# Gated delta stage of a two-block transformer kernel: PSUM banks assigned as a ring, and the next head's preparation moved beside the scan

## What is computed

```
def _gated_delta_chunked(q, k, v, g, beta):
    L = where(strict, einsum(k_beta, k) * decay, 0)
    t_inv = triangular_solve(eye + L, eye)
    u, w = t_inv @ v_beta, t_inv @ (k_beta * exp(g))
    qk = where(tri, einsum(q, k) * decay, 0)
    def step(S, xs):                       # one chunk after the other
        v_new = u_c - w_c @ S
        o = qg_c @ S + qk_c @ v_new
        S = S * dl_c + kd_c^T @ v_new
o = o_fwd + o_bwd;  o = rms_norm(o) * silu(z)
```

## Time and profile before

| | us |
|---|---|
| median of 3 runs (4356.33 to 4364.41) | 4357.08 |
| the profiled execution | 4365.17 |
| its span in the trace | 4363.4 |
| delta stage, from the first level batch (2079.7) to o ready (2738.1) | 658.5 |
| PE busy over the whole span | 3933.6 (90%) |
| DVE busy | 2020.1 (46%) |
| ACT busy | 1886.3 (43%) |
| POOL busy | 1091.2 (25%) |
| mean granted clock of TensorE | 0.946 |

### The profile page before, as it was taken

How to read it: one execution, slowest core, us unless ns; L and a number is a source line. 1 busy time by engine, 2 the same in 40 slices (tenths; PEclk the granted TensorE clock), 3 DMA queues, 4 the chain that set the end, 5 groups by cost and what they waited for, 6 DMA issues and landing times. The chain is left out here.

```text
span 4363.4 us, 54559 instructions
## 1 busy us (share of the span) xinstructions
PE 3933.6 (90%) x20807; PEld 3314.5 (76%) x20807; DVE 2020.1 (46%) x3497; ACT 1886.3 (43%) x3241; POOL 1091.2 (25%) x596
## 2 busy tenths in 40 slices
PE   8989998879959999995878776897999999999998
PEld 6879997757737777874878775797888778888886
DVE  4358874277745222313656567674234233000353
ACT  5248765357746554331434443565324242111232
POOL 0034430010022332211333334122532111212341
PEclk9999998789979999997989887898999999999999
DMA  3744214489954322222221212114643123222342
GB/s 118 258 130 105 51 40 154 173 338 420 420 218 132 97 95 97 74 92 74 54 76 41 77 52 76 52 37 139 221 148 116 44 81 124 80 66 82 128 145 101
DMA packets 337172, 548.35 MB, mean 126 GB/s; under 512 B 117092, under 2 KB 210148, under 8 KB 325860
## 3 DMA queue, kind: packets, MB, share of 16 engines
...
## 5 line engine op out<-in xcount | busy, mean ns | idle before, releaser
L3340 POOL TENSOR_TENSOR end_w_lo<-end_w_raw,end_w_hi 128x1024 fp32r<-128x1024 f32 x144 | 353.6, 2465 | 835.8 <-ACT end_w_hi L3529 835.6
L3772 PE MATMUL end_ps<-end_xT_hi,end_w_hi 128*128 128x512 f32 (+1 forms) x896 | 344.7, 385 | 4.7 <-DVE end_xT_lo L3369 2.4
L3772 PE MATMUL end_ps<-end_xT_lo,end_w_hi 128*128 128x512 f32 (+1 forms) x896 | 342.9, 383 | 0.0
L3772 PE MATMUL end_ps<-end_xT_hi,end_w_lo 128*128 128x512 f32 (+1 forms) x896 | 342.8, 383 | 0.0
L3529 ACT ACTIVATE end_w_hi<-end_w_raw 128x1024 fp32r<-128x1024 f32 x144 | 150.1, 1054 | 268.4 <-PE end_ps L3772 139.9
L2685 POOL TENSOR_TENSOR mid_w_lo<-mid_w_raw,mid_w_hi 128x1024 fp32r<-128x1024 f32 (+1 forms) x64 | 153.0, 2396 | 406.3 <-ACT mid_w_hi L2873 406.3
L3043 PE MATMUL mid_ps<-mid_w_hi,mid_xT_hi 128*128 128x512 f32 x576 | 228.7, 397 | 2.8 <-DVE mid_xT_lo L2747 2.8
L3043 PE MATMUL mid_ps<-mid_w_lo,mid_xT_hi 128*128 128x512 f32 x576 | 224.4, 390 | 0.0
L3043 PE MATMUL mid_ps<-mid_w_hi,mid_xT_lo 128*128 128x512 f32 x576 | 224.4, 390 | 0.0
L3501 DVE TENSOR_TENSOR end_rows<-end_rows,end_ps 128x512 f32<-128x512 f32 x44 | 30.3, 688 | 417.5 <-PE end_ps L3772 417.5
L3772 PE MATMUL end_ps<-end_w_hi,end_xT_hi 128*128 128x512 f32 x544 | 214.4, 394 | 0.0
...
## 6 DMA issues: line engine op xcount, KB each, us to landing
...
```

The lines of the kernel that those rows point to most:

```text
L3340: pool.tensor_tensor(halves(w_lo, piece), w_raw[:, 2 * q:2 * q + 2], halves(w_hi, piece).bitcast(F32), ALU.subtract).then_inc(w_split, 1)
L3772: ins = pe.matmul(o_, lhsT, rhs, start=(k == 0 and part == 0), stop=(k == KC - 1 and part == 2))
```

## The change

- The level batches, and the u and w groups after them, use banks 0 to 4 in a ring: batch i writes bank i mod 5. Bank 5 is free for the preparation, banks 6 and 7 belong to the scan alone (the first head still prepares in 6 and 7). o shares its place with the product for v_new.
- The Gram products of head w+1 move from i = 16, 18, ... to i = 0, 3, 6, 9, beside the scan, each followed on DVE by its `decays` at i = 1, 4, 7, 10. `AQ` gets a third buffer; the freed tile `row_prod` moves into it.
- The transposes of k and v move to i = 24 to 27, all in bank 5, each waiting for ACT's copy of the one before (at i = 25 to 28).
- The elimination moves from i = 30 to 35 to i = 16 to 25, and so does what follows it on SP.
- `spread` and `exponents` run for head w+2 at i = 28 to 35, not for head w+1 beside the scan; those of head 1 run before the first turn.
- SP stores o and loads z ahead of `give_blocks`, not at the end of its turn.
- ACT squares the last o tiles one chunk at a time (i = 10 to 16), `root` moves to i = 22, `decay_rows` to i = 23.

```
-        L, AQ, inv = (st.sb(n, [P, 2, NI, P]) for n in ("L", "AQ", "inv"))
+        L, inv = (st.sb(n, [P, 2, NI, P]) for n in ("L", "inv"))
+        AQ = st.sb("AQ", [P, 3, NI, P])
...
-        turn_bank, half_bank, full_bank = (0, 1, 2, 3), (4, 5, 0, 1), (2, 3, 4, 5)
-        uw_bank = (0, 1, 2, 3, 4, 5, 2, 3)
-        uw_left = (1, 2, 7, 8)
+        RING = 5
+        uw_left = (5, 6, 7, 8)
...
-        PREP = SCANS
+        GRAM_AT, TURN_AT, KEEP_AT = (0, 3, 6, 9), (24, 25, 26, 27), (25, 26, 27, 28)
+        DECAY_AT, SQUARE_AT, SPREAD_AT, EXP_AT = (1, 4, 7, 10), (10, 12, 14, 16), (28, 29, 30, 31), (32, 33, 34, 35)
+
+        def prep_bank(h, j):
+            return 6 + j % 2 if h == 0 else 5
+
+        def scan_place(d, part):
+            return ps[:, 6 + d, part * P:(part + 1) * P]
+
+        def ring_bank(lev, phase, b):
+            return (((lev - 1) * 3 + phase) * NB + b) % RING
+
+        def uw_bank(g):
+            return (BATCHES + g) % RING
 
         def level_of(i):
...
                         if w + 2 < H:
                             load_rows(w + 2)
+                        if w:
+                            store(w - 1)
+                            load_z(w)
                         give_blocks(w + 1)
                         if w + 2 < H:
                             load_qk(w + 2)
...
-                    if w:
...
-                            dve.wait_ge(sd_done, NI * (h - 1))
+                        if h >= 3:
+                            dve.wait_ge(sd_done, NI * (h - 2))
...
+                for b in range(NB):
+                    spread(1, b)
...
-                SOLVED_AT = {BATCHES - 6: range(1, 4), BATCHES - 5: range(4, 7), BATCHES - 4: range(7, 9), BATCHES - 3: range(9, 11),
-                             BATCHES - 2: range(11, 13), BATCHES - 1: range(13, SMALL - 1)}
+                SOLVED_AT = {17: (1, 2), 18: (3, 4), 19: (5, 6), 20: (7,), 21: (8,), 22: (9,), 23: (10,), 24: (11, 12), 25: (13, 14)}
...
-                        if w and i == BATCHES - 10:
+                        if w and i == 26:
                             finish(w - 1)
                         if w + 1 < H:
-                            if i in (2, 5, 8, 11):
-                                spread(w + 1, i // 3)
-                            if PREP < i <= PREP + 4:
-                                decays(w + 1, i - PREP - 1)
-                            if i == BATCHES - 6:
+                            if i in DECAY_AT:
+                                decays(w + 1, DECAY_AT.index(i))
+                            if i == 16:
                                 begin_solve(w + 1)
                             if i in SOLVED_AT:
                                 solve(w + 1, SOLVED_AT[i])
+                            if w + 2 < H and i in SPREAD_AT:
+                                spread(w + 2, SPREAD_AT.index(i))
                         elif i < ROW_STEPS:
                             row_step(i)
                 for c in range(NT):
...
-                def squares(h):
-                    act.wait_ge(o_kept, NI * (h + 1))
-                    for t in range(NT):
-                        ins = act.activation(dump[:, t], o[:, t], ACT.Square, accum_out=osum[:, 0, t:t + 1])
-                    ins.then_inc(osum_done, 1)
+                def squares(h, c):
+                    for d in range(2):
+                        t = chunk_at(c, d)
+                        act.wait_ge(o_kept, NI * h + 2 * c + d + 1)
+                        act.activation(dump[:, t], o[:, t], ACT.Square, accum_out=osum[:, 0, t:t + 1]).then_inc(osum_done, 1)
 
...
-                        if w and i == PREP + 1:
-                            squares(w - 1)
-                        if w and i == PREP + 3:
+                        if w and i in SQUARE_AT:
+                            squares(w - 1, NT // 2 + SQUARE_AT.index(i))
+                        if w and i == 22:
                             root(w - 1)
                         if w + 1 < H:
-                            if i in (4, 7, 10, 13):
-                                exponents(w + 1, i // 3 - 1)
-                            if PREP + 4 < i <= PREP + 8:
-                                keep_tok(w + 1, i - PREP - 5)
-                            if i == BATCHES - 6:
+                            if i == 23:
                                 decay_rows(w + 1)
+                            if i in KEEP_AT:
+                                keep_tok(w + 1, KEEP_AT.index(i))
+                            if w + 2 < H and i in EXP_AT:
+                                exponents(w + 2, EXP_AT.index(i))
...
-                def prepare(h, i):
-                    j = i % 4
-                    if i == 0:
+                def gram(h, j):
+                    if j == 0:
                         pe.wait_ge(qk_in[h % 2], 32 * (h // 2 + 1))
-                        if h >= 2:
-                            pe.wait_ge(S_done, NI * (h - 1))
-                            pe.wait_ge(o_kept, NI * (h - 1))
                         if h:
                             pe.wait_ge(tok_done, 4 * h)
-                    if 2 <= i < 6:
-                        pe.wait_ge(grams_kept, 4 * h + i - 1)
-                    if i >= 6:
-                        pe.wait_ge(tok_done, 4 * h + i - 5)
-                    if i < 4:
...
+                    if h:
+                        pe.wait_ge(grams_kept, 4 * h + j)
+                    elif j >= 2:
+                        pe.wait_ge(grams_kept, j - 1)
+                    for n in range(2):
+                        t = 2 * j + n
+                        ins = pe.matmul(ps[:, prep_bank(h, j), n * 256:n * 256 + 256], qk[:, h % 2, t, 0],
+                                        qk[:, h % 2, t].rearrange("p m c -> p (m c)"), start=True, stop=True)
+                    ins.then_inc(grams, 1)
+
+                def turn_values(h, j):
+                    if h:
+                        pe.wait_ge(grams_kept, 4 * h + 4)
+                        pe.wait_ge(tok_done, 4 * h + j)
+                    elif j < 2:
+                        pe.wait_ge(grams_kept, j + 3)
                     else:
...
+                        pe.wait_ge(tok_done, j - 1)
+                    if j == 2:
+                        pe.wait_ge(v_in, 16 * (h + 1))
+                    for n in range(4):
+                        t = 4 * (j % 2) + n
+                        src = qk[:, h % 2, t, 0] if j < 2 else vT[:, t * P:(t + 1) * P]
+                        ins = turn(pe, bank(prep_bank(h, j))[:, n], src, ident)
+                    ins.then_inc(turned, 1)
...
-                        if w + 1 < H and PREP <= i < PREP + 8:
-                            prepare(w + 1, i - PREP)
+                        if w + 1 < H and i in GRAM_AT:
+                            gram(w + 1, GRAM_AT.index(i))
+                        if w + 1 < H and i in TURN_AT:
+                            turn_values(w + 1, TURN_AT.index(i))
                     pe.wait_ge(bvk_done, 4 * (w + 1))
                     for b in range(NB):
...
                     for b in range(NB):
-                        pe.wait_ge(lev_D, PER * w + NB * (LEVELS - 1) + (b + 1 if b < 2 else NB))
-                        if b == 3:
-                            pe.wait_ge(uw_copied, 8 * w + 4)
...
+                        for m in range(2):
+                            g = 2 * b + m
+                            pe.wait_ge(lev_D, PER * w + NB * (LEVELS - 1) + min(max(b + 1, g), NB))
+                            if g >= RING:
+                                pe.wait_ge(uw_copied, 8 * w + g - RING + 1)
+                            for k in range(4 * b, 4 * b + 4):
+                                left, right = ((kbg, invT) if m else (invT, bv))
+                                ins = pe.matmul(bank(uw_bank(g))[:, k % 4], left[:, k], right[:, k], start=True, stop=True)
+                            ins.then_inc(uw_done, 1)
```

95 lines of the change are left out of this document (41 added, 54 removed).

## The result

The changed kernel takes 4371.38 us (median of 12 runs), the kernel before 4363.77 us in runs on the same chip: a ratio of 1.0016, 95% interval 1.0009 to 1.0023. It is slower by 7.6 us, in the band that the forecast called "the same". In the profiled executions it is 6.7 us of span (4370.1 against 4363.4), and the delta stage holds more than all of it. Windows of the changed kernel: head 0, heads 1 to 6, the last head to its scan's end, and from there to TensorE's next work; then two stretches inside head 4. The columns are those of the earlier trace rows.

A forecast was written before the change was run, and what follows sets the result against it. Some 20 us a head of waits, latencies and slow clock above PE's 53 us of work. Head 0 +2.2, heads 1 to 6 -7.1, last head -3.3, end -1.9 sum to -10.1: 4347 us, range 4341 to 4354.

The forecast's parts named there:

- (a): From a steady head's first Gram batch to the scan's end: 27.5 us of PE work, 31.5 with 4 us of waits.
- (b): POOL's kd and qg after the scan take 8.5 us, to 40.2; the elimination gets one instruction per POOL instruction.
- (c): Rest of the elimination, with extends and POOL's relate, takes 12.7 us, to 52.9; PE's waits meanwhile are off this chain.
- (d): Previous head's closing product to 55.3, then masks and extends: u and w start at 60.8, PE through at 67.9.
- (e): SP stores o, loads z and writes the inverted blocks behind them: 6.3 us, to 61.6.
- (f): Scatter issues, then q and k land: 10.1 us, to 71.7; PE, back at 69.2, waits 2.5 us.
- I add 0.8 us: Allowance for low clock from the wait for q and k before the scan, between nothing and 5 us.
- The four cycles forecast at 72.5 us: Steady cycles within heads 1 to 6, from one first Gram batch to the next: 72.5 us each, against 72.9.
- Head 0: First head: masks against POOL, Gram wait for k and q, extends held up; 54.7 in place of 52.5, +2.2 us.
- The last head: First row tile, which DVE waits for, is issued 3.3 us earlier relative to the head: -3.3 us.
- the self-feeding wait for q and k: Rival: a wait over 3 us before the first Gram batch lowers TensorE's clock; cycle 76.8, 4369 us; chance 0.27.
- PE becomes the bound: Rival: the elimination gets through beside POOL, so a head is PE's 65 us; 4307 us; chance 0.12.

The follow-up runs named there:

- the small products: Changed kernel with GpSimd's kd and qg of heads 1 to 7 computed for 8 of 128 columns only, so not the full function: 4317.36 us.
- Filling the gaps: Changed kernel with q and k issued earlier, plus added TensorE products of no use during its waits in heads 1 to 6: 4351.39 us, ratio 0.9972.
- masks-first kernel: Changed kernel with the other runs' edits joined, finish behind the last masks, diagonal blocks' load ahead of the store: 4293.27 us, ratio 0.9843.

## Why the prediction was wrong

By its own steps, in the head whose first Gram batch is at 2358.21, measured from there:

- (a) Scan's end at 31.5 us: 32.1. Right.
- (b) GpSimd through at 40.2, one elimination instruction per product: 41.0 and 7.4 us for four instructions. Right, and shown by the small products.
- (c) Elimination's end at 52.9 with a wait of 5 us for the masks and three of 1.35 us: 53.3, 5.2 and 1.22 to 1.27. Right.
- (d) `finish` to 55.3: 55.9. Then **"u and w start at 60.8 and PE is through at 67.9"**: 65.1 and 72.2. This is the step that failed. VectorE was free for the last masks nearly in time (its spreads ended at 60.7, forecast 60.1), but TensorE's product for them was not there: 1.84 us of waiting on VectorE's side. The forecast said of the wait for the masks and of the gaps between the turned tiles "Neither is on this chain", and let u and w follow VectorE alone. TensorE's own arm, which it never added up, is by its own prices 31.5 + 8 x 0.89 + 5 + 8 x 0.44 + 3 x 1.35 + 8 x 0.89 = 58.3, ahead of 60.8. So the gaps alone would not have made it the longer one. Of the 6.7 us that it came later, 0.9 had gathered by the end of the wait (44.5), and 5.9 came behind it: 20.6 us where these prices, at full clock, give 14.7.
- (e) Scatter from 61.6: 62.5. Right.
- (f) q and k landed at 71.7: 72.4. Right. The wait of 2.5 us that should follow did not show, because TensorE came later than they did.
- The term behind both: **"I add 0.8 us"** for the clock, placed at q and k. The 5 us wait that the forecast itself had in (c) was given no clock, although stood there for a shorter wait. Those 5.9 us are its price on TensorE's arm in this head. Filling the gaps gave back 4.5 us a head on that arm, and 2.9 us of cycle before the last masks bound again. In the masks-first kernel, where the other arms are shorter too, low clock is absent and TensorE's busy time is 5.4 us a head less.

The four cycles forecast at 72.5 us came out at 73.5 on average, which is nearly right, but by luck: the forecast's number came from the queue's arm (72.4 us to the landing of q and k), and TensorE's, for which it had 69.2, was the longer one. It shows where only TensorE's path counts. From head 6's first Gram batch to head 7 the forecast had 67.5 and the trace has 72.3 us. Heads 1 to 6 missed by 9.4 us: 4.4 in the five cycles, 4.8 there, 0.2 at the start.

Head 0 missed by 5.4 us (+7.7 for +2.2). Its waits were named, but not priced one by one. TensorE was idle 3.3 us longer there and busy 4.4 us longer for the same products, and the clock of the stretch fell from 0.92 to 0.80: (1 - 0.80) x 2 x 60.13 is 24 us of low clock against 8 before. With two banks for the turned tiles head 0 took 6.1 us less, at a clock of 0.87; waits and clock were not separated here. The end was right: 2.0 for 1.9 us. The last head missed by 4.0: TensorE waited 10.56 us where 9.71 stood before, not less. The forecast took the landing of the first row tile for the cause, and in the kernel before it was: GpSimd waited 4.13 us for it (at 2580.84). In the changed kernel the tile is there, but VectorE's first row step waits for GpSimd, which squares the tile behind four products for `bv` and `kbg` and one for z, and begins those only when u and w are done:

```profile
2589.44 1.49 DVE L1703 TENSOR_REDUCE delta_row_stat<-delta_GB 128x10 f32<-128x1280 f32 x1 [10.43 <-POOL delta_GB L1554]
```

```profile
2577.37 1.90 POOL L1528 TENSOR_TENSOR delta_bv<-delta_tok,delta_vec 128x1024 f32<-128x1024 f32 x1 [31.57 <-PE delta_ps L1979]
...
2587.08 2.32 POOL L1554 TENSOR_TENSOR delta_GB<-delta_qk 128x1280 f32<-128x1280 f32 x1
```

An earlier tile can't help there. A kernel with that square taken ahead wasn't tried. The four misses make 18.7 us; the 1.9 us outside the stage bring them to the 16.8 between -10.1 and the measured +6.7 of the traces.

The rule on transfers that the prediction weighed, from the Trainium skill's page "DMA: Bandwidth & Descriptors", section "Anatomy of one DMA — SWDGE (gpsimd) path", is a fit to transfers that GpSimd issues, which the prediction didn't say; those of this stage are issued by SyncE. It fits the small ones here: 16 KB of diagonal blocks landed after 2.1 us (median of 48). It doesn't fit q and k, 5.0 us (median of 10) against an estimate of 3.2, and the measured time was the right one to take.

Of the rivals, the self-feeding wait for q and k named a time near the result, 4369, by a mechanism that isn't there: TensorE waited for q and k once, 0.5 us, and q and k much earlier changed 4.4 us. Its parts do show in the kernel with the elimination behind the masks, and below the 3 us of waiting that it asked for: behind 1.96 us of waiting for q and k, at 2346.48, the granted clock is 0.61 over 4.4 us. "PE becomes the bound" came nearer to the mechanism, but at 73 us a head, not at 65.
